# Neighbourhood attention: split scores, three units in flight, pairs staged a lap ahead, bias laid out with its mask, pointwise bias by VectorE

## The reference

```python
q = axial_rope(to_heads(p[..., OFF_B_Q:OFF_B_K]), rows_pos, cols_pos)   # 16 heads of 64
k = axial_rope(to_heads(p[..., OFF_B_K:OFF_B_V]), rows_pos, cols_pos)
# a query sees 16 columns around its own in all 4 rows, and the whole context:
s_loc = einsum('bwhd,bawkhd->bhwak', q_r * hd ** -0.5, k_win) + bias
s_ctx = einsum('bwhd,bchd->bhwc', q_r * hd ** -0.5, kc)
p = softmax(concatenate([s_loc, s_ctx]))
out = p_loc @ v_win + p_ctx @ vc
# layer 0 alone: the context's own queries attend to the context
s = einsum('bqhd,bchd->bhqc', qc * hd ** -0.5, kc); na_c = softmax(s) @ vc
# convolution branch
y = layer_norm(depthwise_conv(glu(u)));  yc = (silu(y) @ conv_pw + conv_pw_b) * silu(gate)
```

## Time and profile before

| | |
|---|---|
| median of 3 runs (lowest, highest) | 3490.7 us (3485.49, 3494.09) |
| profiled execution, its time and its span | 3488.28 us, 3486.2 us |
| mean granted clock of PE | 0.985 of full speed |
| layer 0: last projection ends, first scores, last values end | 2446.7, 2486.3, 2630.7 us |
| layer 1: the same | 3247.0, 3266.8, 3373.4 us |
| POOL adds the mask (L2345) | 2461.4 to 2475.6, 3262.1 to 3276.6 us |

### The profile page before, as it was taken

How to read it: one execution, slowest core, us unless ns; L and a number is a source line. 1 busy time by engine, 2 the same in 40 slices (tenths; PEclk the granted TensorE clock), 3 DMA queues, 4 the chain that set the end, 5 groups by cost and what they waited for, 6 DMA issues and landing times.

```text
span 3486.2 us, 40825 instructions
## 1 busy us (share of the span) xinstructions
PE 3388.2 (97%) x15230; PEld 2724.6 (78%) x15230; DVE 2281.0 (65%) x4121; ACT 1547.3 (44%) x2894; POOL 45.0 (1%) x50
## 2 busy tenths in 40 slices
PE   9999999999998999999999999999999989999998
PEld 7888878888887888887887888888567766888666
DVE  6888887777765888888776335555464346645655
ACT  5444444456655544444555222222353344422454
POOL 0000000000000000000000000000100000000100
PEclk9999999999999999999999999999899999999899
DMA  7777777775546777777874333333103245534224
GB/s 263 257 260 256 250 266 240 261 244 173 154 158 197 256 258 258 262 257 259 265 265 165 93 91 96 98 97 97 52 1 121 74 139 146 169 97 119 102 70 160
DMA packets 285001, 613.77 MB, mean 176 GB/s; under 512 B 18882, under 2 KB 21506, under 8 KB 282884
## 3 DMA queue, kind: packets, MB, share of 16 engines
q1 hardware_dynamic: 280804, 596.26, 52.9%
q0 software_dynamic: 2048, 9.37, 0.8%
q10 hardware_dynamic: 1952, 5.54, 0.5%
HBM read 604.80 MB, written 6.29 MB: 175 GB/s over the span
## 4 chain that ended last, share of the span: by engine, by line
PE 80%; DVE 9%; DMA 6%; ACT 4%; issue 2%; ACTq 0%; SPq 0%; DVEq 0%
PE acc L401 24%; PE acc L403 23%; PE acc L402 23%; DMA raw<-ffn_w_gu 6%; DVE lo L396 3%; PE acc L2207 2%; PE acc L2181 2%; ACT hi L392 1%; DVE cgw L1151 1%; DVE mw L1153 1%; PE tp L2194 1%; PE tp L2158 1%; PE tp L1823 0%; DVE tm L1713 0%; DVE rn L1613 0%
## 5 line engine op out<-in xcount | busy, mean ns | idle before, releaser
L396 DVE TENSOR_TENSOR lo<-raw,hi 128x512 fp32r<-128x512 f32 x1808 | 1209.1, 689 | 931.3 <-ACT hi L392 923.8
L392 ACT ACTIVATE hi<-raw 128x512 fp32r<-128x512 f32 x1808 | 1116.6, 630 | 1581.1 <-PE acc L403 1296.6
L401 PE MATMUL acc<-hi,hT_hi 128*128 128x512 f32 x1760 | 702.8, 399 | 28.5 <-DVE hT_lo L1138 12.7
L401 PE MATMUL acc<-hi,h_hi 128*128 128x512 f32 x1696 | 674.9, 398 | 22.1 <-DVE lo L396 17.6
L402 PE MATMUL acc<-hi,hT_lo 128*128 128x512 f32 x1760 | 687.7, 391 | 0.0
L403 PE MATMUL acc<-lo,hT_hi 128*128 128x512 f32 x1760 | 687.6, 391 | 0.0
L403 PE MATMUL acc<-lo,h_hi 128*128 128x512 f32 x1696 | 663.0, 391 | 0.0
L402 PE MATMUL acc<-hi,h_lo 128*128 128x512 f32 x1696 | 662.3, 391 | 0.0
L401 PEld LDWEIGHTS acc<-hi,hT_hi 128*128 128x128 f32 x1760 | 331.2, 188 | 121.0 <-DVE hT_lo L1138 22.1
L401 PEld LDWEIGHTS acc<-hi,h_hi 128*128 128x128 f32 x1696 | 319.5, 188 | 102.4 <-DVE lo L396 32.1
L403 PEld LDWEIGHTS acc<-lo,hT_hi 128*128 128x128 f32 x1760 | 331.6, 188 | 70.5
(11 more groups left out here) (278 smaller groups left out, 2340.7 us busy)
## 6 DMA issues: line engine op xcount, KB each, us to landing
raw<-ffn_w_gu SPq DMA_DIRECT2D x352, 512.0 KB, 5.5
raw<-w_in SPq DMA_DIRECT2D x280, 512.0 KB, 3.8
mw<-wmt SPq DMA_DIRECT2D x192, 512.0 KB, 5.2
raw<-ffn_w_down SPq DMA_DIRECT2D x176, 512.0 KB, 5.3
raw<-w_out SPq DMA_DIRECT2D x96, 512.0 KB, 4.1
ball<-rpbx SPq DMA_DIRECT2D x8, 768.0 KB, 8.5
x_rest<-x POOLq DMA_DIRECT2D x2, 2048.0 KB, 9.9
x<-x_rest SPq DMA_DIRECT2D x2, 2048.0 KB, 7.7
```

What stands on the lines that cost most here:

```text
L392: act.activation(hi[:, g % RING, :], raw_piece(g), ACT.Copy).then_inc(S["hi_made"], 1)
L396: dve.tensor_tensor(lo[:, g % RING, :], raw_piece(g), hi[:, g % RING, :].bitcast(F32), ALU.subtract).then_inc(S["lo_made"], 1)
L401: pe.matmul(bank, act_hi, hi[:, slot, :], start=start, stop=False)
```

## The change

- **Scores** are made of three float32r products, as in the projections. `T` is replaced by two pairs of tiles, `Th` (high parts, copied by ACT: `hi_q`, `hi_k`) and `Tl` (what is left, subtracted by DVE from `cg` in PSUM: `lo_q`, `lo_k`).
- **Three units in flight.** Scores, maximum and exponential run for unit k+2 in step k. The scores go in turn to `acc[0]`, `acc[1]` and `tp[1]`, and `pr`, `nm` and `sm` have three slots. The transposes of all units go to `tp[0]`, so `na_turn` waits also until ACT has copied those of the unit before.
- **Pairs are staged a lap ahead.** The pair after the next gets its rope at k = 1 and 2 (one call each; `lo_q` and `lo_k` of the next pair stand ahead of the first), its transposes at k = U-1, its high parts at k = U; pairs 0 and 1 ahead of the first step.
- **Bias.** The mask is put into the bias array beforehand; the load of `mask`, POOL's additions and `bias_ready` go.
- **Pointwise bias.** `cpb` is loaded into all 128 partitions (256 KB instead of 2 KB) and added by DVE in `conv_gate`, in halves of 256 columns, each then multiplied with the gate. `conv_gate(t)` comes one tile later in DVE's order.

```diff
-        T = at("T", H + 4 * K1, [P, 2 * CH])
-        pr = at("pr", H + 8 * K1, [P, 2, CH])
+        Th = [at(f"Th{k}", H + (4, 35)[k] * K1, [P, 2 * CH], F32R) for k in range(2)]
+        Tl = [at(f"Tl{k}", H + (31, 23)[k] * K1, [P, 2 * CH], F32R) for k in range(2)]
+        pr = [at(f"pr{k}", H + (8, 10, 21)[k] * K1, [P, CH]) for k in range(3)]
...
+        def s_bank(n):
+            return (acc[0], acc[1], tp[1])[n % 3]
...
-                sp.dma_start(cpb[:], a["conv_pw_b_2"][ly:ly + 1, :]).then_inc(S["cf_in"], 16)
+                sp.dma_start(cpb[:], row_bc(a["conv_pw_b_2"][ly:ly + 1, :], CH)).then_inc(S["cf_in"], 16)
...
-                sp.dma_start(mask[:], a["mask"]).then_inc(S["na_in"], 16)
...
+                def hi_q(pair):
+                    act.wait_ge(S["cg_done"], cgs + 2 * pair + 1)
+                    act.activation(Th[pair % 2][:, 0:nt * P], cg[0][:, 0:nt * P], ACT.Copy,
+                                   scale=NA_D ** -0.5).then_inc(S["th_made"], 1)
...
                 def step(lap, k, end):
-                    if k == 1 and end > U:
-                        stage_ctx(lap, 1)
-                    if k + 1 < end:
-                        na_exp(lap, k + 1)
-                    if k == U - 2 and end > U:
-                        take_k(lap, 1)
+                    if k + 2 < end:
+                        na_exp(lap, k + 2)
+                    if (lap, k) == (0, 1):
+                        hi_q(1)
+                        hi_k(1)
+                    if k == U and lap < 6:
+                        hi_q(lap + 2)
                     if k < end:
                         na_pt(lap, k)
+                    if k == U and lap < 6:
+                        hi_k(lap + 2)
+                    if k == 1 and lap < 6:
+                        stage_ctx(lap, 2)
...
+                def lo_q(pair, ly=ly, nt=nt):
+                    dve.wait_ge(S["th_made"], 16 * ly + 2 * pair + 1)
+                    dve.scalar_tensor_tensor(out=Tl[pair % 2][:, 0:nt * P], in0=cg[0][:, 0:nt * P], scalar=NA_D ** -0.5,
+                                             in1=Th[pair % 2][:, 0:nt * P].bitcast(F32), op0=ALU.mult,
+                                             op1=ALU.subtract).then_inc(S["cg_taken"], 1)
...
                 def step(lap, k, end):
                     na_sum(lap, k - 1)
-                    if k == 1 and end > U:
-                        rope(lap, 1, 0)
-                    if k + 1 < end:
-                        na_max(lap, k + 1)
-                    if k == U - 2 and end > U:
-                        take_q(lap, 1)
+                    if k + 2 < end:
+                        na_max(lap, k + 2)
+                    if k == 1 and lap < 7:
+                        lo_q(lap + 1)
                     na_out(lap, k - 1)
-                    if k == 1 and end > U:
-                        rope(lap, 1, 1)
+                    if k == 1 and lap < 7:
+                        lo_k(lap + 1)
+                    if k == 1 and lap < 6:
+                        rope(lap, 2, 0)
+                    if k == 2 and lap < 6:
+                        rope(lap, 2, 1)
...
-                    dve.tensor_tensor(gC[:, t], tp[t % 2][:], gC[:, t], ALU.mult).then_inc(S["yc_made"], 1)
+                    for k in range(2):
+                        cols = slice(k * L, (k + 1) * L)
+                        ins = dve.tensor_tensor(r2[k], tp[t % 2][:, cols], cpb[:, cols], ALU.add)
+                    link(ins)
+                    for k in range(2):
+                        cols = slice(k * L, (k + 1) * L)
+                        ins = dve.tensor_tensor(gC[:, t, cols], r2[k], gC[:, t, cols], ALU.mult)
+                    ins.then_inc(S["yc_made"], 1)
...
-                    if t >= 1:
-                        conv_gate(t - 1)
+                    if t >= 2:
+                        conv_gate(t - 2)
+                conv_gate(nt - 2)
+                lo_q(0)
+                lo_k(0)
                 conv_gate(nt - 1)
-                take_q(0, 0)
                 na_max(0, 0)
                 na_max(0, 1)
+                rope(0, 1, 0)
+                rope(0, 1, 1)
+                na_max(0, 2)
...
-                    pe.matmul(tp[t % 2][:], ones[0:1, :], cpb[:], start=False, stop=True).then_inc(S["pw_done"], 1)
...
+                    pe.wait_ge(S["p_made"], 16 + u0 + n - 2)
...
+                        pe.matmul(dst, qh[r, qs], qh[r, ks], start=True, stop=False)
+                        pe.matmul(dst, ql[r, qs], qh[r, ks], start=False, stop=False)
+                        ins = pe.matmul(dst, qh[r, qs], ql[r, ks], start=False, stop=True)
...
                 def na_turn(lap, u):
                     pe.wait_ge(S["p_made"], lap * U + (16 + u0 + u + 1))
+                    wait(pe, "pt_taken", lap * U + u0 + u)
...
                 def step(lap, k, end):
-                    if k + 1 < end:
-                        na_scores(lap, k + 1)
-                    if k == U - 2 and end > U:
-                        staged(lap, 1)
+                    if k + 2 < end:
+                        na_scores(lap, k + 2)
+                    if (lap, k) == (0, 1):
+                        staged(0, 1)
+                    if k == U - 1 and lap < 6:
+                        staged(lap, 2)
                     if k < end:
                         na_turn(lap, k)
                     na_values(lap, k - 1)
...
-                for pair in range(NA_H // 2):
-                    bv = bias[:, 2 * pair:2 * pair + 2].rearrange("p h (r n) -> p (h r) n", n=GRID)
-                    pool.tensor_tensor(bv, bv, mask[:].unsqueeze(1).broadcast_to([P, 12, GRID]), ALU.add)\
-                        .then_inc(S["bias_ready"], 1)
```

More of the change, by code:

```diff
@@ L79, in pool_matrices @@
     return m.reshape(len(POOLS), 2, P, L).transpose(2, 1, 0, 3).copy()
[L82 to L88, removed]
 def bias_rows(rpb):
     q, k = np.arange(GRID)[:, None], np.arange(GRID)[None, :]
+    first = np.clip(q - 8, 0, GRID - 16)
     cols = np.clip(k - q + RPB_C // 2, 0, RPB_C - 1)
@@ L977, in _, with hi_k @@
                     ins.then_inc(S["s_made"], 1)
[L980 to L982 removed]
+                def hi_q(pair):
+                    act.wait_ge(S["cg_done"], cgs + 2 * pair + 1)
+                    act.activation(Th[pair % 2][:, 0:nt * P], cg[0][:, 0:nt * P], ACT.Copy,
+                                   scale=NA_D ** -0.5).then_inc(S["th_made"], 1)
+                def hi_k(pair):
+                    act.wait_ge(S["cg_done"], cgs + 2 * pair + 2)
+                    act.activation(Th[pair % 2][:, CH:2 * CH], cg[1][:], ACT.Copy).then_inc(S["th_made"], 1)
                 def na_exp(lap, u):
                     act.wait_ge(S["m_ready"], lap * U + (16 + u0 + u + 1))
+                    n = lap * U + u
+                    rows = pr[n % 3]
                     if kinds[u % U][1] < 2:
[L988 to L989 removed]
+                        act.activation(rows[:], rows[:], ACT.Exp, bias=nm[:, n % 3, 0:1], scale=-1.0,
+                                       accum_out=sm[:, n % 3, 0:1]).then_inc(S["p_made"], 1)
                     else:
                         for t in range(2):
[L992 to L994 removed]
+                            cols = slice(t * L, (t + 1) * L)
+                            ins = act.activation(rows[:, cols], s_bank(n)[:, cols], ACT.Exp, bias=nm[:, n % 3, t:t + 1],
+                                                 accum_out=sm[:, n % 3, t:t + 1])
                         ins.then_inc(S["p_made"], 1)
@@ L1629, in na_max @@
                         if u % U == 0:
[L1630 removed]
+                            dve.wait_ge(S["bias_in"], 64 * (ly + 1))
                             dve.wait_ge(S["nil_made"], ly + 1)
@@ L1647, in na_sum @@
                     dve.wait_ge(S["o_taken"], lap * U + (ot0 + u - 1))
-                    link(dve.reciprocal(rr[:, u % 2], sm[:, u % 2]) if kinds[u % U][1] == 2 else
-                         dve.reciprocal(rr[:, u % 2, 0:1], sm[:, u % 2, 0:1]))
+                    n = lap * U + u
+                    link(dve.reciprocal(rr[:, u % 2], sm[:, n % 3]) if kinds[u % U][1] == 2 else
+                         dve.reciprocal(rr[:, u % 2, 0:1], sm[:, n % 3, 0:1]))
                 def na_out(lap, u):
@@ L2177, in na_scores @@
                         pe.wait_ge(S["cg_taken"], lap * 2 + (cgs + 2 * (u // U) + 2))
-                    pe.wait_ge(S["p_made"], lap * U + (16 + u0 + u - 1))
-                    if t < 2:
-                        ins = pe.matmul(acc[u % 2][:], T[r, t * P:(t + 1) * P], T[r, CH:2 * CH], start=True, stop=True)
-                    else:
-                        for tt in range(2):
-                            ins = pe.matmul(acc[u % 2][:, tt * L:(tt + 1) * L], T[r, L + tt * P:L + (tt + 1) * P],
-                                            T[r, CH + L:2 * CH], start=True, stop=True)
+                    n = lap * U + u
+                    pe.wait_ge(S["p_made"], 16 + u0 + n - 2)
+                    qh, ql = (v[(lap + u // U) % 2] for v in (Th, Tl))
```

(15 more changed lines are left out.)

62 lines of the change are left out of this document (37 added, 25 removed).

## The result

The changed kernel takes 3564.1 us, median of four runs (3556.4 to 3566.4), against 3489.6 (3485.5 to 3494.1) for the kernel before in the same job: ratio 1.0214, 95% interval 1.0191 to 1.0237. It is slower, by 2.1%, and 11 us above the predicted 3553. The profiled span is 3564.6 us.

The account below looks back on a forecast made before the run. PE was taken to set the pace, with DVE not far behind; new idle would drop its clock. Layer 0's +35 and layer 1's +30 us on the profiled execution's 3488.3 gave 3553 us, 8-in-10 range 3468 to 3578.

Parts of the forecast that it names:

- The mechanism: Both attention stages: late maxima delay pt and idle PE, 2.0 and 2.4 us once a lap, so the clock falls; chance 0.57.
- PE idle for 2.0 us at transposes 3: Layer 0 lap: maximum 4 waits behind DVE's rope, so pt 2 comes late and PE idles 2.0 us before transposes 3.
- idle 2.4 before the staging: Layer 1 lap: staging of the pair after next waits for rope's second half until 7.1, PE through at 4.7.
- Low-clock unit: One attention unit at 1.2 GHz: 4.65 us less 2.00 for the old scores plus 1.28 for three products, 3.93 us.
- slack rival: Both attention stages: subtractions and rope are absorbed, so laps are PE-bound at 13.9 us (layer 0) and 9.5 (layer 1).
- Layer 0's sum: Layer 0 attention: first values at 2485.8, low-clock units and stagings, less 17 for returns, end at 2666 against 2630.7: +35 us.
- The returns: Layer 0: full clock comes back two or three times behind a joined staging, each worth four units at 1.8, 7 us.
- Layer 1's sum: Layer 1 attention: first values at 3272.5, low-clock units and stagings, one return of 5 us, end at 3404 against 3373.4: +30 us.
- The head: Start of the stages: mask and pointwise-bias changes bring the first values 8.1 us earlier in layer 0, 1.05 in layer 1.
- The clock holds: Rival: clock stays full after each stage's start; laps 17.7 and 12.2 us, -4 us per layer, time 3480; chance 0.22.
- the slack is there: Rival of the other sign: -26 us in layer 0, -20 in layer 1, time 3442; chance 0.11.
- Low throughout: Rival: clock stays low over both stages with no return, +52 us in layer 0, +35 in layer 1, time 3575; chance 0.10.

Follow-up runs that it names:

- a_swap: Changed kernel with ACT's copy of the transposes (pt k) ahead of the exponential of unit k+2 and the high copy of Q: 3483.0 us, ratio to before 0.9986.
- b_plain: Changed kernel with one plain fp32 score product in place of the three split ones, low halves still made but not read: 3542.9 us, ratio to before 1.0161.
- e_twice: Changed kernel with the first of the three score products issued twice, scores staying the same: 3574.9 us, ratio to before 1.0253.
- g_heads: Kernel before with only the bias laid out with its mask and the pointwise bias added by DVE: 3469.1 us, ratio 0.9951.
- d_bias: Kernel before with only the bias laid out with its mask, without POOL's additions: 3486.7 us, ratio 1.0005.
- i_stage: h_lo with, in layer 1, staging one unit later and the low half of Q ahead of maximum 3: 3439.3 us, ratio to before 0.9857.
- c_split: Kernel before with the split scores alone, keeping its own order, two units in flight and its own staging: 3606.6 us, ratio 1.0358.
- h_lo: a_swap with, in layer 1, the low half of K ahead of the output product in DVE's order: 3474.7 us, ratio to before 0.9966.

## Why the prediction was right

**The mechanism.** Confirmed for the falls inside the laps. In layer 0 PE's idle ahead of its transposes, released by pt, ends every return to full clock, and then the clock stays low through work without gaps. a_swap takes that one wait away and brings layer 0 from 46 us behind to 26 ahead, with no fall after the first return; b_plain and e_twice leave it and stay at 3543 and 3575. The rule weighed in the prediction (the Trainium skill, TensorE: Matmul & The Clock Gate, Why this matters for your kernels) would have kept the clock in all of these laps; the trace disagrees, with 0.85 us of idle at 2588.

**What stayed open in it.** The longest low stretch, 102 us from 2480.4, holds no wait for pt after its start. It began behind a wait for rope at the head:

```profile
2480.08 1.73 PE L2213 MATMUL cgw<-ident,st 128*128 128x128 f32 x8 [1.24 <-DVE st L1627]
```

From 2485 to 2503 PE does the same work in a_swap, each start some 0.3 us later. There the clock came back at 2503.4, here at 2582.8. So in these two profiles the order decides what becomes of a return, and not when it comes. That the clock would stay low for long was taken from the earlier trace rows, from experience and not from a cause, and the runs give no cause either.

**Which idle.** The step "PE idle for 2.0 us at transposes 3" was never reached in layer 0: all three returns are lost at the lap's start, by the idle that the step put at 1.0 and that measured 0.85. The statement that this decides was right, the size of the idle needed was drawn too large from the earlier trace rows. In layer 1, "idle 2.4 before the staging" measured 0.24 at low clock.

**Low-clock unit: mis-sized.** 3.93 was predicted, 4.22 measured. Timeline of PE, from one unit's scores to the next:

```profile
2485.13 0.79 PE L2231 MATMUL acc<-Th 64*128 64x512 f32 x1
2485.72 0.62 PE L2232 MATMUL acc<-Th,Tl 64*128 64x512 f32 x1
2486.15 0.62 PE L2233 MATMUL acc<-Tl,Th 64*128 64x512 f32 x1
2486.70 1.11 PE L2245 MATMUL tp<-ident,pr 128*128 128x128 f32 x4
2487.61 1.81 PE L2258 MATMUL acc<-qkvg,pt 128*128 128x64 f32 x8
2489.35 0.58 PE L2231 MATMUL tp<-Th 64*128 64x256 f32 x1
```

The three products take 0.59 + 0.43 + 0.55 = 1.57 us to the transposes, not 3 x 0.43 = 1.28: in the earlier trace rows the split products stand in an unbroken stream, here each triple follows and precedes another kind. At 44 and 28 scores behind the first values 0.29 is 13 us in layer 0 and 8 in layer 1. At full clock the same (a_swap): 0.33 + 0.24 + 0.32 = 0.89, not 0.68, a context unit 0.90 and not 0.72; so a unit is 2.32 us with no wait at all (a_swap), not 2.12. The slack rival's laps, 13.9 us, could not have been had.

**Layer 0's sum.** Predicted +35, measured +45.6. The scores add 13 us, and the head was 2.4 us better (first values at 2483.4, predicted 2485.8). The returns were too dear by 5: there were three, as allowed, but each held three units and a wait, and by its rows was worth 4.0 us and not 7. The other way, the sum counted 47 whole units where 44 scores and 46 transposes were left, and a staging adds 1.70 us and not 1.90: 6 us together. That the total came within 11 us of the measured one is in part such terms cancelling.

**Layer 1's sum.** Predicted +30, measured +32.7. A wait was missed: the scores of each new pair behind the low half of K.

```profile
3371.18 0.76 PE L2231 MATMUL acc<-Th 64*128 64x512 f32 x1 [0.97 <-DVE Tl L1641]
...
3377.26 1.54 PE L2213 MATMUL cgw<-ident,st 128*128 128x128 f32 x6 [0.25 <-DVE st L1627]
```

It is worth 0.97 x 7 = 7 us, and with the mis-sized scores 15. Stagings with 0.25 us of idle instead of 0.65 and a shorter hand-over give back 4, the parts of units counted too often 5, and the full clock 4: two returns of 4.2 and 3.5 us, and the last 2 us of the stage (1.5), where 5 was assumed.

**The head.** Predicted 8.1 us earlier in layer 0, measured 10.3 (2483.4 against 2493.7); in layer 1 1.05, measured 1.7 from the last values of layer 0. g_heads shows these parts' gain by itself, 19 us. Its profile has 10 us of low clock in layer 1 in place of 34, but 51 in layer 0 in place of 24. That an undisturbed rope is worth 5 us could not be shown: d_bias is within its uncertainty of before. In the changed kernel rope's first operation is 0.41 to 0.43 us throughout, so the cause is gone, but it lay where the clock was low anyway. By the Trainium skill (SBUF — State Buffer, Who interferes with whom) a VectorE instruction with two inputs in SBUF contends with a GpSimd instruction that reads SBUF. The trace agrees: rope's first operation reads `qkvg` and `ropn`; the one that ran beside GpSimd's additions took 1.42 us, and without them none took over 0.43.

**Rivals.** *The clock holds* (3480) and *the slack is there* (3442) fall for the kernel as changed. With its waits taken out (i_stage) both are nearly true: 3439 us, PE-bound laps of 14.8 and 10.2 us. *Low throughout* (3575) is as near the measured 3564 as the forecast is; what stands between are short returns, three in layer 0 and two in layer 1. So the run speaks for the clock's fall in every lap that holds full clock, and hardly tells these two apart by its time alone.

## What to carry over

Where an engine works its queue in order, the short operation that frees a single buffer (here pt, which empties the only transposes bank) belongs ahead of the long chain for a later unit; lookahead that is queued in front of it is paid by the engine that waits for the bank. On TensorE price a wait by the clock it can cost: 0.85 to 1.6 us of idle a lap cost 8 to 12 us a lap here (layer 0's laps of 23 to 27 us in the changed kernel against 14.8 in a_swap, 27.3 in c_split against 16.95 before), so read the granted clock by stretches, not the busy share. Price a short run of small products by rows with the same neighbours, not by the spacing in a long stream.

## What was not expected of the hardware

An idle stretch does not cost the clock by its length alone. Lost: behind 0.85 or 0.86 us three times (changed kernel, layer 0) and behind 1.57 us in each lap of c_split. Kept: the laps of the kernel before, where at full clock PE waited seven times for an exponential in layer 0, and five times for rope in layer 1, by 0.86 or 0.87 us each:

```profile
PE tp L2194 <- ACT pr L992: 4.6, 7, 0.7
```

```profile
PE cgw L2169 <- DVE st L1614: 4.3, 5, 0.9
```

h_lo's layer 1 kept it through three laps of 0.9 and 0.4 us and lost it in the fourth. In layer 0 of b_plain and e_twice five returns outlived a first wait of 0.6 to 0.7 us and ended behind the next, of 1.1 to 1.3 us. So no length that costs the clock can be given from these runs: 0.85 us lost it in one kernel and 0.87 kept it in another, in laps of different work. Chance has its part: the 3.14 us at 1109 that cost the kernel before nothing is there in the changed kernel too, as 2.78 us, and there the clock is low from 1108.2 to 1111.6.

Once low it stayed so for up to 102 us although PE was busy for 99% of them, and for 51 us with a fourth product a unit as well (e_twice). What brings it back was not isolated: in the changed kernel each return in layer 0 stands behind a staging joined to transposes, but three of its six such stagings brought none; and h_lo, whose layer 0 has a_swap's code, was low for 3.4 us at the head where a_swap was for 24. Kernels differ in their spread from run to run (over ten runs 33 us in d_bias, 34 in h_lo, 19 in a_swap; 11 in five of i_stage, 10 in four of the changed kernel); with so few runs it can't be tied to the idle stretches.
